# Splitting the columns of a triangular inverse between two engines

## What is computed

```
m = jnp.where(strict, jnp.einsum('nbhid,nbhjd->nbhij', kb, kc) * gam, 0.0)
t_mat = m + jnp.eye(L)
rhs = jnp.concatenate([vc * bc[..., None], kb * jnp.exp(g)[..., None]], axis=-1)
sol = lax.linalg.triangular_solve(t_mat, rhs, left_side=True, lower=True, unit_diagonal=True)
...
def step(s, inp):            # one chunk after the other
    v_new = u_i - w_i @ s
    o_i   = (q_i * exp(g_i)) @ s + a_i @ v_new
    s     = s * exp(g_last) + (k_i * exp(g_last - g_i)).T @ v_new
```

## Time and profile before

| what | value |
| --- | --- |
| median of 3 runs | 2305.11 us |
| lowest and highest run | 2305.1 us, 2309.77 us |
| span of the profiled execution | 2304.5 us |
| PE, DVE, ACT, POOL busy in it | 2104.7, 742.9, 493.4, 163.7 us |
| share of the chain that ended last | PE 78%, DMA 10%, DVE 8%, issue 2%, ACT 1% |

### The profile page before, as it was taken

One profiled execution on the slowest core, in us unless ns is written; L12 is line 12 of the kernel. 1 busy time (PEld: TensorE's weight loads), 2 busy tenths in 40 slices (PEclk: granted clock), 3 DMA queues, 4 the chain that ended last, 5 costly groups with the idle time before them and its releaser, 6 DMA issues.

```text
span 2304.5 us, 33012 instructions
## 1 busy us (share of the span) xinstructions
PE 2104.7 (91%) x13898; PEld 1069.9 (46%) x13898; DVE 742.9 (32%) x1394; ACT 493.4 (21%) x1159; POOL 163.7 (7%) x139
## 2 busy tenths in 40 slices
PE   5998999838799889999999989999999599999997
PEld 3544666538794323333333334553774244444442
DVE  2143535587763411111010131000772411111113
ACT  2223446535561110000000021000551100000001
POOL 0000005311110001100111000000000000000000
PEclk7999999967689989999999999999999799999999
DMA  7119765442235379999999971110204599999996
GB/s 294 63 53 362 256 199 205 149 170 103 75 133 189 122 282 365 402 394 404 397 393 394 405 289 65 55 37 33 95 30 193 206 401 420 420 420 420 420 421 272
DMA packets 120157, 576.50 MB, mean 250 GB/s; under 512 B 13984, under 2 KB 26784, under 8 KB 72528
## 3 DMA queue, kind: packets, MB, share of 16 engines
q1 hardware_dynamic: 111904, 546.94, 60.2%
q0 software_dynamic: 7168, 23.83, 3.6%
q10 hardware_dynamic: 944, 3.67, 0.4%
HBM read 537.85 MB, written 34.96 MB: 249 GB/s over the span
## 4 chain that ended last, share of the span: by engine, by line
PE 78%; DMA 10%; DVE 8%; issue 2%; ACT 1%; SPq 0%; DVEq 0%; POOLq 0%; ACTq 0%
PE ps L2396 24%; PE ps L2408 5%; PE ps L510 5%; DMA work_sb<-expert_w_up 4%; PE ps L1887 4%; PE ps L938 4%; PE ps L2765 3%; PE ps L1928 2%; PE ps L2737 2%; PE ps L2746 2%; PE ps L2426 2%; PE ps L2446 2%; DMA ring_sb<-expert_w_up 2%; DMA ring_sb<-ada_w 2%; PE ps L937 2%
## 5 line engine op out<-in xcount | busy, mean ns | idle before, releaser
L2396 PE MATMUL ps<-work_sb 128*32 128x512 f32 (+1 forms) x2416 | 424.1, 596 | 7.6 <-DMA work_sb<-expert_w_up 5.2
L2396 PE MATMUL ps<-ring_sb,work_sb 128*32 128x512 f32 (+1 forms) x1984 | 285.4, 598 | 13.1 <-DMA ring_sb<-expert_w_up 6.5
L2396 PEld LDWEIGHTS ps<-work_sb 128*32 128x32 f32 (+1 forms) x2416 | 128.5, 120 | 218.6 <-issue 215.6
L2396 PEld LDWEIGHTS ps<-ring_sb,work_sb 128*32 128x32 f32 (+1 forms) x1984 | 81.8, 117 | 190.6 <-issue 181.3
L2587 DVE TENSOR_TENSOR work_sb<-ps,work_sb 128x512 f32<-128x512 f32 x32 | 20.6, 686 | 435.8 <-PE ps L2408 331.1
L2518 ACT ACTIVATE work_sb<-ps 128x1024 f32<-128x1024 f32 x16 | 16.4, 1024 | 512.8 <-PE ps L2408 294.1
L510 PE MATMUL ps<-ring_sb,work_sb 128*128 128x512 f32 (+1 forms) x288 | 108.1, 537 | 0.9 <-DVE work_sb L405 0.9
L2528 ACT COPY work_sb<-ps 128x512 f32<-128x512 f32 x32 | 17.3, 589 | 406.0 <-PE ps L2484 406.0
L2408 PE MATMUL ps<-work_sb 128*32 128x512 f32 x768 | 101.6, 597 | 0.0
L2408 PE MATMUL ps<-ring_sb,work_sb 128*32 128x512 f32 x768 | 101.0, 597 | 0.0
L938 PE MATMUL ps<-work_sb,ring_sb 128*128 128x512 f32 x192 | 98.0, 592 | 0.0
(11 more groups left out here) (436 smaller groups left out, 3023.6 us busy)
## 6 DMA issues: line engine op xcount, KB each, us to landing
work_sb<-expert_w_down SPq DMA_DIRECT2D x70, 1024.0 KB, 14.6
work_sb<-expert_w_gate SPq DMA_DIRECT2D x68, 1024.0 KB, 10.9
work_sb<-expert_w_up SPq DMA_DIRECT2D x68, 1024.0 KB, 14.8
ring_sb<-expert_w_gate SPq DMA_DIRECT2D x52, 1024.0 KB, 8.9
ring_sb<-expert_w_up SPq DMA_DIRECT2D x50, 1024.0 KB, 12.1
ring_sb<-expert_w_down SPq DMA_DIRECT2D x50, 1024.0 KB, 15.2
ring_sb<-ada_w SPq DMA_DIRECT2D x96, 512.0 KB, 6.6
ring_sb<-wout SPq DMA_DIRECT2D x16, 512.0 KB, 6.3
```

The lines of the kernel that those rows point to most:

```text
L2396: mm = pe.matmul(ps[g:g + wide, bank + n, :], lat_src[:, k, g:g + wide], us[e][:, n * 512:(n + 1) * 512], start=(k == 0), stop=(k == KT - 1))
```

## The change

VectorE keeps columns 0 to 7 of WB in every step (SPLIT = 8), and POOL does columns 8 to j in steps 8 to 30, with the same two instructions for each step on its own scratch OUTER_P. Columns don't depend on one another, so neither engine reads what the other writes; only the two transposes at the end need both. VectorE still issues 62 instructions for each group, with k min(j + 1, 8) elements; POOL issues 46, with k(j - 7) elements. Each POOL instruction waits for the one before it (`pool_step`).

`end` waits for POOL's columns ahead of the transposes. The first transpose reports by `dve_first`, which POOL's columns wait for. On POOL's queue the new work stands behind `zero_pool(0)` for group 0, behind `levels_pool(0)` and ahead of the first four `keys_pool` for group 1, and behind `levels_pool(1)` and ahead of `keys_pool(4)` for group 2. Each of the eight copies of `levels_pool` now reports by itself, and POOL waits for them ahead of its columns of groups 1 and 2. Two semaphores are shared with earlier uses under new names (`sT_zero` is `pool_step`, `dve_eps` is `dve_first`).

```diff
@@ regions
-        OUTER = region(11264, 256)
+        SPLIT = 8
+        OUTER, OUTER_P = region(11264, SPLIT * 31), region(11520, 256)
@@ levels_pe
-                pe.wait_ge(dn_wd, g + 1)
+                pe.wait_ge(dn_wd, 8 * (g + 1))
@@ class Inverse
             def __init__(self, dve, g, step):
-                self.g, self.step, self.done = g, step, 0
+                self.dve, self.g, self.step, self.done = dve, g, step, 0
                 dve.wait_ge(dn_ra, g + 1)
                 dve.wait_ge(dn_eye, 2 * (g + 1))
                 blocks = H[:, 4:6, 0:512].rearrange("p t (m c) -> p c t m", c=32)
-                step(nc.vector.transpose(NB.rearrange("p c (t m) -> p c t m", t=2), blocks))
+                nc.vector.transpose(NB.rearrange("p c (t m) -> p c t m", t=2), blocks).then_inc(dve_first, 1)
+                dve.wait_ge(dve_first, g + 2)
 
             def steps(self, count):
                 for j in range(self.done, min(self.done + count, 31)):
-                    k = 31 - j
-                    o = OUTER[:, 0:k * (j + 1)].rearrange("p (i c) -> p i c", i=k)
-                    self.step(nc.vector.tensor_tensor(o, bc(NB[:, j + 1:32, j:j + 1], [P, k, j + 1]),
-                                                      bc(WB[:, j:j + 1, 0:j + 1], [P, k, j + 1]), ALU.mult))
-                    self.step(nc.vector.tensor_tensor(WB[:, j + 1:32, 0:j + 1], WB[:, j + 1:32, 0:j + 1], o, ALU.subtract))
+                    k, n = 31 - j, min(j + 1, SPLIT)
+                    o = OUTER[:, 0:k * n].rearrange("p (i c) -> p i c", i=k)
+                    self.step(nc.vector.tensor_tensor(o, bc(NB[:, j + 1:32, j:j + 1], [P, k, n]),
+                                                      bc(WB[:, j:j + 1, 0:n], [P, k, n]), ALU.mult))
+                    self.step(nc.vector.tensor_tensor(WB[:, j + 1:32, 0:n], WB[:, j + 1:32, 0:n], o, ALU.subtract))
                     self.done = j + 1
 
             def end(self):
                 self.steps(31)
+                self.dve.wait_ge(pool_step, pool_steps(self.g + 1))
@@ new on POOL
+        def pool_steps(groups):
+            return 1 + 2 * (31 - SPLIT) * groups
+
+        def late_columns_pool(pool, g):
+            pool.wait_ge(dn_eye, 2 * (g + 1))
+            pool.wait_ge(dve_first, g + 2)
+            if g > 0:
+                pool.wait_ge(dn_wd, 8 * g)
+            at = pool_steps(g)
+            for j in range(SPLIT, 31):
+                k, n = 31 - j, j + 1 - SPLIT
+                o = OUTER_P[:, 0:k * n].rearrange("p (i c) -> p i c", i=k)
+                nc.gpsimd.tensor_tensor(o, bc(NB[:, j + 1:32, j:j + 1], [P, k, n]),
+                                        bc(WB[:, j:j + 1, SPLIT:j + 1], [P, k, n]), ALU.mult).then_inc(pool_step, 1)
+                pool.wait_ge(pool_step, at + 1)
+                w = WB[:, j + 1:32, SPLIT:j + 1]
+                nc.gpsimd.tensor_tensor(w, w, o, ALU.subtract).then_inc(pool_step, 1)
+                pool.wait_ge(pool_step, at + 2)
+                at += 2
@@ dn_pool
             eye_pool(pool, 0)
             zero_pool(0)
+            late_columns_pool(pool, 0)
             eye_pool(pool, 1)
             levels_pool(pool, 0)
+            late_columns_pool(pool, 1)
             for i in range(4):
                 keys_pool(pool, i)
             eye_pool(pool, 2)
             levels_pool(pool, 1)
+            late_columns_pool(pool, 2)
             keys_pool(pool, 4)
             keys_pool(pool, 5)
```

More of the change, by code:

```diff
@@ L210, in build @@
         s_silu = sem("s_silu")
-        sT_zero = sem("sT_zero")
+        pool_step = sem("pool_step")
         rows_in = sem("rows_in")
@@ L348, in root_table @@
         def root_table(act):
-            act.wait_ge(dve_eps, 1)
+            act.wait_ge(dve_first, 1)
             nc.scalar.activation(stat_t[:, 30:31], EPSC, ACT.Sqrt)
@@ L419, in norm_pe @@
                 tr.then_inc(tr_ok, 1)
-        dve_eps = sem("dve_eps")
+        dve_first = sem("dve_first")
         SMALL_IN = 2
@@ L1666, in levels_pool @@
                 for d in range(2):
-                    last = nc.gpsimd.tensor_copy(w[r, d, :, :, 32 * b:32 * b + 32], diag((VUP, VLO)[d], d)[r])
-            last.then_inc(dn_wd, 1)
+                    nc.gpsimd.tensor_copy(w[r, d, :, :, 32 * b:32 * b + 32], diag((VUP, VLO)[d], d)[r]).then_inc(dn_wd, 1)
         def keys_pool(pool, i):
@@ L3095, in _ @@
             nc.vector.memset(EPSC, EPS)
-            nc.vector.memset(ONE, 1.0).then_inc(dve_eps, 1)
+            nc.vector.memset(ONE, 1.0).then_inc(dve_first, 1)
             nc.vector.memset(A[:, :, CTX:LO], 0.0)
@@ L3124, in _ @@
             act.wait_ge(small_in, 32)
-            act.wait_ge(sT_zero, 1)
+            act.wait_ge(pool_step, 1)
             nc.scalar.activation(sT[:, :, 0:2], cT.rearrange("p (k v) -> p k v", v=2), ACT.Silu).then_inc(s_silu, 1)
@@ L3148, in _ @@
         def _(pool):
-            nc.gpsimd.memset(sT_t[:, :], 0.0).then_inc(sT_zero, 1)
+            nc.gpsimd.memset(sT_t[:, :], 0.0).then_inc(pool_step, 1)
             pool.wait_ge(am_ok, KT)
```

## The result

The changed kernel takes 2313.5 us (median of 11 runs, 2308.84 to 2322.12), the kernel before 2306.16 us (11 runs, 2302.44 to 2312.36). The ratio is 1.0033 with a 95% interval of 1.0022 to 1.0044: slower by 5 to 10 us. The profiled execution of the changed kernel has a span of 2320.3 us and is the longest of its runs, so its span is no measure of the change; its stretches are.

What follows compares the result with a forecast made beforehand. VectorE was taken to bound group 0's inverse and the early steps of groups 1 and 2. Group terms of +0.1, +1.0 and +0.4 us summed to +1.5 us, 2306.6 us on the median; range 2302 to 2318.

Steps and rivals of the forecast that it cites:

- the likeliest case: Inverses of all groups: VectorE and POOL in lockstep, POOL near 0.24 us fixed an instruction; 2306.6 us, chance 0.53.
- rival (a): POOL's columns, all groups: its instructions cost more than 0.24 us fixed; about +10 us, 2315 us, chance 0.34.
- a POOL at 0.17 us of wait: POOL's columns: 0.17 instead of 0.06 us between instructions, 24.9 us a group; upper bound 25.8 us, 2318 us.
- the two engines exclude one another while they read: Inverse columns: while one engine works through its SBUF elements the other does not; only fixed parts overlap.
- (b): Inverse columns: short instructions of both engines slip past each other; -8.2 us, 2297 us, chance 0.09.
- (c): Inverse columns: engines exclude each other for whole instructions, fixed parts too; +39 us, 2344 us, chance 0.04.
- The pace: Inverse columns: while POOL runs, VectorE gets about one instruction for each of POOL's; group 0 takes 23.5 us.
- undisturbed 18.6 us: Group 0's inverse: VectorE's 62 smaller instructions take 18.6 us if nothing disturbs them, 4.8 us less than before.
- POOL's fixed cost: POOL's columns: 0.18 us fixed plus 0.06 us wait for each of 46 instructions, 19.8 us a group with elements.
- decision point: POOL's cost for one instruction: from 0.262 instead of 0.24 us on, the kernel is slower by over 4.6 us.
- The keys behind the columns: Groups 1 and 2: key products queued after POOL's columns block VectorE twice, 1.45 us; their delay is covered.
- a shift as carried 1:1: After the inverses: the output product and experts' weights follow, so a shift here reaches the end in full.

Runs made afterwards that it cites:

- the second comparison of the two kernels: The unedited changed kernel, measured again against the kernel before: 2312.62 us against 2307.82, ratio 1.0026.
- POOL writing: Changed kernel with POOL's 46 instructions a group made fills that read nothing, columns 8 to 31 not computed: 2293.61 us, ratio 0.9940.
- the delay: Kernel before, plus five VectorE products of 256 elements ahead of group 1's scan, nothing on POOL: 2311.45 us against 2307.78, ratio 1.0020.
- POOL alone: Changed kernel without VectorE's 62 instructions a group, columns 0 to 7 not computed: single run, time not compared; POOL's 46 took 20.81 us.

## Why the prediction was right or wrong

The median of 2313.5 us lies within the range of 2302 to 2318, but the likeliest case was not the one that came. I forecast 2306.6 us, no change that can be measured; what came is rival (a), at +7.3 us, between my +1.5 and its +10. Of these 7.3 us the columns explain 4.9, just over the 4.6 us from which (a) counts. The other 2.4 us have no cause that is shown, and the second comparison of the two kernels (+4.8 us) doesn't need them. That the upper part of the range, made for a POOL at 0.17 us of wait, took in the result is in part luck.

- That the two engines exclude one another while they read, which I took from the earlier trace rows, is shown: POOL beside VectorE costs it 6 us in group 0, POOL writing costs it nothing. Rivals (b) and (c) are out. At full exclusion group 0 would have taken 38.4 us; it took 24.5. The Trainium skill, SBUF — State Buffer, section SBUF: two separate sides, has the shared pair of ports held for the whole instruction; the runs show that the fixed parts overlap.
- The pace is shown for this split, one instruction of VectorE for one of POOL's: I had said that VectorE has done about 46 when POOL ends, with 3.7 us left; it was in its 47th, with 3.5 us left. Its undisturbed 18.6 us came as 18.56.
- The step that failed is POOL's fixed cost: 0.18 + 0.06 = 0.24 us, from instructions of 512 and 1024 elements and from a wait between two fills. It measured 0.27 us, of which 0.08 between two instructions, and with slightly cheaper elements POOL took 20.88 us instead of 19.8. This was the decision point that I had named for rival (a), 0.262. Through the pace the 1.1 us went one for one into each group: +1.15, +2.20 and +1.51 us against my +0.1, +1.0 and +0.4, which is 3.4 us over the forecast of 1.5.
- The keys behind the columns blocked VectorE twice as I had it: steps of 80 and 72 elements took 1.09 and 0.96 us. Their delay cost nothing, nor did the wait in `end`, since POOL ended 3.5 us ahead of VectorE, nor the renamed semaphores: with group 0 alone split no difference could be measured (-2.8 to +2.3 us).
- What I left out is TensorE's clock. I took the scans as fixed and a shift as carried 1:1. The scan of group 1 took 2.3 us more in one profile and 4.8 in the other. That a later start of the scan costs more than its lateness is supported by the delay (2.3 us of delay, 3.4 in the stretch), but with group 0 alone split and with POOL alone the scan was slow after a short wait; neither cause nor size is settled.
- The first profile of the changed kernel is 15.8 us longer in span than that of the kernel before. 8.5 us of this lie after the gather at 815.97 us, up to the idle issue time at 1357.88, in the stage that waits for the experts' weights. The second profile of the changed kernel needed 530.9 us for the same stretch, the two of the kernel before 533.4 and 534.7, so these 8.5 us did not come again and are no effect of the change that can be shown.

## What to carry to other kernels

Before work moves from VectorE to GpSimd beside it, look whether both take their operands from SBUF. If they do as here, their elements exclude one another and only the fixed parts overlap, so two chains of dependent instructions run one for one at the pace of the slower. What still paid is a share so small that GpSimd's elements pass in the fixed time between VectorE's instructions: here columns 12 or 16 onwards, not 8. It gave some 3 us; leaving columns 8 onwards out altogether gave 14. Price a chain of small dependent GpSimd instructions from a small dependent one, or put the uncertainty of its fixed cost times their number into the likeliest case.

## What the runs showed of the hardware

- POOL alone and POOL beside VectorE took the same 20.8 and 20.9 us for 46 instructions of up to 144 elements: of the two, only VectorE lost. With at most 64 elements POOL lost too: 15 elements took it 0.36 and 0.39 us instead of 0.22 and 0.23.
- An instruction of VectorE with one input from SBUF (TENSOR_SCALAR, 769 elements) took 0.62 us alone and 2.69 us beside a POOL product.
- A dependent product or subtraction on POOL costs 0.27 us and 1.7 to 2.0 ns for each element; the same on VectorE 0.19 us and 1.04 ns. A dependent fill on POOL of 143 elements took 0.22 us.
- The same 16 products at the start of group 1's scan took 2.00 us (twice), 2.41 and 2.59, and 3.67 or 3.68 us in kernels that hardly differ there, at a granted clock of 1.00 or 0.79, 0.79, and 0.50 to 0.64 over the 8 us from their start. A profile's difference of 2 us in such a stretch is no sign of a change by itself.
